# The end of a full-row product: the last two chunks taken bank by bank

## The reference

```python
x = layer_norm(DN_ALPHA * x + mix, ...)              # mix = h @ pw2_w + b; later attention @ b_wo
x = layer_norm(DN_ALPHA * x + (silu(g) * u) @ w_down + ple, ...)   # FFN_DIM 2816
h = (silu(h @ w_gate) * (h @ w_up)) @ w_down         # blocks 2: before an RMS norm
x = x + 0.5 * rms_norm(h, ff1_norm_post)
h = concat(o_diff, o_nsa) @ w_out
x = x + rms_norm(h, mix_norm_post)
```

## Time and profile before

| | |
|---|---|
| median of 3 runs | 2543.68 us (2541.88 to 2545.12) |
| the profiled execution, its own time | 2544.07 us |
| its span, first to last instruction | 2542.3 us |
| mean granted TensorE clock | 0.991 of 2.4 GHz |
| TensorE busy | 2448.5 us, 96% of the span |
| VectorE, ScalarE, GpSimd busy | 38%, 39%, 38% |

### The profile page before, as it was taken

How to read it: one execution, slowest core, us unless ns; L and a number is a source line. 1 busy time by engine, 2 the same in 40 slices (tenths; PEclk the granted TensorE clock), 3 DMA queues, 4 the chain that set the end, 5 groups by cost and what they waited for, 6 DMA issues and landing times.

```text
span 2542.3 us, 30518 instructions
## 1 busy us (share of the span) xinstructions
PE 2448.5 (96%) x11142; PEld 1930.3 (76%) x11142; DVE 953.9 (38%) x1165; ACT 981.6 (39%) x1520; POOL 968.2 (38%) x422
## 2 busy tenths in 40 slices
PE   8999999999999999999999999999899889999997
PEld 6866788888677776788888588888577656788885
DVE  6974244420422215344401433310556763333202
ACT  7754333322466634333322522222334563322212
POOL 5733444444323223444444244444232103444442
PEclk9999999999999999999999999999999999999999
DMA  4212223333111112333333133333322002223322
GB/s 144 67 41 66 88 95 99 97 93 96 61 58 59 52 57 75 94 96 99 94 96 93 56 92 98 99 91 99 124 67 67 26 1 67 90 93 99 92 98 74
DMA packets 57062, 206.70 MB, mean 81 GB/s; under 512 B 6304, under 2 KB 6304, under 8 KB 56736
## 3 DMA queue, kind: packets, MB, share of 16 engines
q1 hardware_dynamic: 56016, 199.96, 25.0%
q10 hardware_dynamic: 976, 5.77, 0.6%
HBM read 203.61 MB, written 2.10 MB: 81 GB/s over the span
## 4 chain that ended last, share of the span: by engine, by line
issue 59%; POOL 22%; PE 13%; DVE 4%; POOLq 0%; ACT 0%; DMA 0%; SPq 0%; DVEq 0%
POOL wL L370 21%; PE banks L430 4%; PE banks L431 4%; PE banks L432 4%; DVE banks L1512 2%; DMA raw<-ws 0%; POOLq L369 0%; POOL pool_sum L385 0%; DVE gpad L1496 0%; DVE banks L1507 0%; POOLq L397 0%; DVE tmp L1586 0%; DVE tmp L1594 0%; DVE tmp L1517 0%; DVE xf L1597 0%
## 5 line engine op out<-in xcount | busy, mean ns | idle before, releaser
L370 POOL TENSOR_TENSOR wL<-raw,wH 128x1024 fp32r<-128x1024 f32 x369 | 905.1, 2455 | 1524.8 <-ACT wH L948 1524.8
L430 PE MATMUL banks<-xH,wH 128*128 128x512 f32 x2104 | 832.7, 396 | 34.7 <-DVE xL L1403 11.6
L432 PE MATMUL banks<-xH,wL 128*128 128x512 f32 x2104 | 821.0, 390 | 0.0
L431 PE MATMUL banks<-xL,wH 128*128 128x512 f32 x2104 | 820.4, 390 | 0.0
L948 ACT ACTIVATE wH<-raw 128x1024 fp32r<-128x1024 f32 x371 | 392.7, 1058 | 1090.9 <-PE banks L432 1083.7
L430 PEld LDWEIGHTS banks<-xH,wH 128*128 128x128 f32 x2104 | 395.9, 188 | 137.9 <-issue 17.6
L431 PEld LDWEIGHTS banks<-xL,wH 128*128 128x128 f32 x2104 | 396.1, 188 | 83.7 <-issue 3.4
L432 PEld LDWEIGHTS banks<-xH,wL 128*128 128x128 f32 x2104 | 395.8, 188 | 84.0
L430 PE MATMUL banks<-hH,wH 128*128 (+1 forms) x704 | 276.6, 393 | 3.5 <-DVE tmp L1470 3.5
L431 PE MATMUL banks<-hL,wH 128*128 (+1 forms) x704 | 276.3, 393 | 0.0
L432 PE MATMUL banks<-hH,wL 128*128 (+1 forms) x704 | 273.9, 389 | 0.0
(11 more groups left out here) (248 smaller groups left out, 2233.0 us busy)
## 6 DMA issues: line engine op xcount, KB each, us to landing
raw<-ws SPq DMA_DIRECT2D x371, 512.0 KB, 3.5
w1b<-w ACTq DMA_DIRECT2D x2, 2048.0 KB, 11.5
xf<-xT SPq DMA_DIRECT2D x8, 256.0 KB, 7.1
out<-xf SPq DMA_DIRECT2D x8, 256.0 KB, 2.0
pf<-pT ACTq DMA_DIRECT2D x2, 512.0 KB, 4.3
con<-consts SPq DMA_DIRECT2D x1, 637.0 KB, 7.0
par<-params SPq DMA_DIRECT2D x1, 564.5 KB, 8.0
ropeT<-rope ACTq DMA_DIRECT2D x1, 512.0 KB, 4.3
```

The source lines that it names most:

```text
L370: pool.tensor_tensor(wL[:, j, :], raw[:, j, :], fp(wH[:, j, :]), ALU.subtract).then_inc(low_ready, 1)
L430: pe.matmul(bank, wH[:, slot, cols], rh, start=start, stop=False)
L431: pe.matmul(bank, wH[:, slot, cols], rl, start=False, stop=False)
L432: return pe.matmul(bank, wL[:, slot, cols], rh, start=False, stop=stop)
```

## The change

Each full-row product now leaves its last two chunks to a new function. The chunks before them run as they did. The last two are taken bank by bank: bank 0 gets the three matmuls of chunk nk-2 and the three of chunk nk-1, then bank 1, and so on. The waits for both chunks stand ahead of all of it. The two `chunk_done` signals come at bank 7, three matmuls apart. The loop has other bounds: 4 + 4 x 4 + 2 chunks in place of 1 + 5 x 4 + 1 for nk = 22, and 2 + 4 + 2 in place of 3 + 4 + 1 for nk = 8.

```diff
+TAIL = 2
...
-                def one_k(k, j, first=False, last=False):
+                def one_k(k, j, first=False):
...
-                        mm = three(ps[n][:], (slot, slice(n * P, n * P + P)), rh, rl, first, last)
-                        if last and n < 7:
+                        mm = three(ps[n][:], (slot, slice(n * P, n * P + P)), rh, rl, first, False)
+                    mm.then_inc(chunk_done, 1)
+
+                def last_chunks():
+
+                    pe.wait_ge(low_ready, c0 + nk)
+                    pe.wait_ge(ready, ready_base + nk)
+                    for n in range(8):
+                        for k in range(nk - TAIL, nk):
+                            mm = three(ps[n][:], ((c0 + k) % SLOTS, slice(n * P, n * P + P)), rH[:, k, :], rL[:, k, :],
+                                       False, k == nk - 1)
+                            if n == 7:
+                                mm.then_inc(chunk_done, 1)
+                        if n < 7:
                             mm.then_inc(bank_done, 1)
-                    mm.then_inc(chunk_done, 1)
-
-
-                before = 1 + (nk - 2) % SLOTS
-                steps = (nk - 1 - before) // SLOTS
+
+                before = 1 + (nk - 1 - TAIL) % SLOTS
+                steps = (nk - TAIL - before) // SLOTS
...
-                for k in range(before + steps * SLOTS, nk):
-                    one_k(k, k, last=k == nk - 1)
+                last_chunks()
```

## The result

The changed kernel takes 2550.55 us, median of 18 runs (2548.99 to 2554.86), and the kernel before 2543.22 us beside it (18 runs, 2540.94 to 2547.16). The ratio is 1.0028, 95% interval 1.0021 to 1.0035: slower by 0.28%, 7.3 us. The forecast was 2546.9, a change within 0.2%. The profiled execution took 2551.09 us.

The account below looks back on a forecast made before the run. TensorE, busy 2448.5 of 2542.3 us, bounds the kernel, so only tails can change. Terms -2.8 + 4.8 + 1.0 + 0.1 = +3.1 (unrounded +3.2) gave 2546.9 us; own range 2544.5 to 2548.5, 8 in 10 2542.5 to 2550.0.

Parts of the forecast that it names:

- The gains: Tails of pw2, down0, down1, down3: the mean's third sum directly follows the second, 0.65 to 0.74 us each, -2.8 in all.
- eleven operations of 0.6 to 0.7 us: Tail of down0: VectorE is late because it has these for eight banks that come complete 0.68 us apart.
- wout: Tail of wout: late rounding delays the squares, 3.6 us, and GpSimd's split stretches VectorE's first add, 1.2: 4.8 lost.
- down2: Tail of down2: ScalarE waits for the product's end anyway; the split holds the first add slightly, 0.1 us lost.
- the weights' slack: Last two chunks, waited for together: 1.7 us of slack left, cost 0; rival of late weights, 2549, chance 0.03.
- wo: Tail of wo: the late DMA of pf delays the mean's subtraction, 1.0 us lost; 2.0 if slower, 0 at best.
- The clock: Rival: TensorE's new gaps behind wout and wo's mean bring half clock, up to 2.6 us each; slower, chance 0.17.
- spaced sums have slack: Argument against the clock rival: half clock on TensorE's spaced sums in the tails need not cost time.
- the slower DMA: Upper end of the range: the DMA of pf in wo slower by as much again, 2.0 us lost.

Follow-up runs that it names:

- the signal alone: The kernel before, own order of matmuls, with only the chunk_done of chunk nk-2 given two matmuls before each full-row product's end: 2558.74 against 2543.79 us, ratio 1.0058.
- the squares put first: The changed kernel with ScalarE's last rounding of wout put behind its eight squares: 2543.30 against 2543.99 us, ratio 0.9996.
- the held split with the clock kept up: The changed kernel with dummy matmuls in TensorE's gaps at wout and wo, and GpSimd's split behind wout held back: 2545.74 against 2543.78 us, ratio 1.0007.
- the early load: The changed kernel with the DMA of pf issued ahead of wo's chunk stream: 2546.43 against 2543.99 us, ratio 1.0009.
- the run with the split held back: The changed kernel with GpSimd's split at the end of wout held until VectorE's third add of squares: 2549.46 against 2543.79 us, ratio 1.0019.
- both repairs: The changed kernel with wout's squares ahead of ScalarE's last rounding and the load of pf ahead of wo's chunks: 2539.23 against 2543.99 us, ratio 0.9977.
- kept busy: The changed kernel with 20 dummy matmuls in TensorE's gap behind wout and 18 behind the mean of wo: 2547.37 against 2543.99 us, ratio 1.0018.

## Why the prediction was wrong

*The gains* (-2.8): right in size, and the reason is only half right. -0.75, -0.84, -0.83 and -0.78 make -3.2, each 0.1 more than forecast: between its third sum and L494, TensorE took 0.96 us for 0.86 us of work before (657.22 to 658.18 in down0), and this is gone too. The prediction put VectorE's lateness down to eleven operations of 0.6 to 0.7 us. It overlooked that one of them was longer, in pw2, down0, wo and down1 alike. In down0 before:

```profile
650.60 2.42 POOL L370 TENSOR_TENSOR wL<-raw,wH 128x1024 fp32r<-128x1024 f32 x1 [3.01 <-ACT wH L948]
...
652.13 1.43 DVE L1385 TENSOR_TENSOR tmp<-xf 128x512 f32<-128x512 f32 x1
...
658.18 1.88 PE L494 MATMUL banks<-xf,con 128*128 128x512 f32 x4
```

GpSimd's split stretches VectorE's first pair sum from 0.68 to 1.43 us. In the run with the signal alone, same order of matmuls, no split lies there:

```profile
653.24 0.68 DVE L1392 TENSOR_TENSOR tmp<-xf 128x512 f32<-128x512 f32 x1
```

Its third pair sum starts 1.20 us behind the last matmul, and 1.96 before. Without the stretch the third pair sum of the earlier trace rows would have ended near 656.4, just in time for TensorE at 656.48 (an estimate from these rows). So in the layer norm tails most of the gain is the end of that meeting; in down3, where no split is near, the reason given holds. The size came out right because it was read from TensorE's rows and did not depend on the reason. That holding the split would give the same gain in the old order was not run.

*wout* (+4.8): right, +4.68, and both parts of it are shown: the hold by the squares put first, the 1.2 us of the split by the held split with the clock kept up.

*down2* (+0.1) and the weights' slack: right. No stop inside the last 48 matmuls of a product shows.

*wo* (+1.0): the step was right, and 0.3 short at full clock: the subtraction starts 6.84 us behind the last matmul, 5.56 before, so +1.28. From the issue of the DMA to `pH` it took 5.22 us, not 4.95. The other 1.69 of its +2.97 is the clock.

*The clock, which the sum had at 0 and the rivals at 0.17*: this is the step that failed. At full clock the tails add up to -3.2 + 1.28 + 0.09 + 4.68 = +2.85, close to the forecast sum of +3.2. The measured 7.3 has 4.5 more. I had argued from one gap, down2's, where the fall of the clock was free because VectorE set the pace, and that spaced sums have slack. In wo the fall lay on sums that ScalarE and TensorE pace, and there it cost 1.69 us: the profile shows it, and it is gone both when the gap is filled and when the early load shortens it. The rival had up to 2.6 us for each of the two places. In wout's own tail it was free, as argued, until the run with the split held back, where it lasted into L539's sums. Down2's gap isn't always free either, as the profile with both repairs shows.

The other 2.8 us are not shown to that degree. In the profile they lie between the tails (2.5 us), in stretches of half clock behind gaps that the change left as long as they were: 2.19 us ahead of the matmuls that follow `ple`, 2.79 behind down1, 2.49 behind wout. In the profile before, the first of the two gaps of 2.19 was followed by a stretch at half clock (near 293 us) and the second wasn't, and in the profile after it was the other way round (near 1035 us). The pass behind wout began at the half clock in the changed kernel, in two kernels whose stall in wout was gone or filled (squares first, kept busy) and in two whose stall was left (the load ahead, the signal alone); it did not in the kernel before and the other five. Such places move about 1.6 us from run to run. One profile of each kernel does not tell how often each place falls; only the medians do, and by them filling the two gaps takes back 3.9 us, give or take 3. How the new gaps bring more half clock further on stays open, and so does whether they do.

The bounds of the prediction's own range don't quite follow from its terms: 1.0 and 1.2 below 2546.9 is 2544.7, and the slower DMA 1.0 above it is 2547.9, where it has 2544.5 and 2548.5. It doesn't bear on the miss.

## What to carry to other kernels

A completion signal usually has more than one listener: before delaying it, read in program order what stands behind each wait on it, on every engine, and whether a transfer is among it. Here a reordering worth 4.8 us became a loss of 7.3, because the signal that frees a weight slot also stood ahead of two urgent pieces of ScalarE's work; moving those two ahead of it was worth 12.1. A third such piece, in down2, had stood behind the stream before the change as well, and moving it gave 7.2 more. A new gap on TensorE has to be priced twice: for its length, and for the clock behind it. In wo the second price was 1.7 us, where TensorE paced the work; in the changed kernel's sums behind wout, where VectorE did, it was nothing.

## What the runs showed of the hardware

In the places read here, a 128x512 VectorE operation on two SBUF inputs that meets a GpSimd split of 2.3 to 2.6 us ends 0.55 us behind the split's end, wherever it started: 0.7 us alone, it took 1.43 in down0 before (started 1.5 us behind the split), 1.91 in wout after, 2.80 in down0 with the signal alone, 2.43 for the first of the two of `pL` (3.03 is both). Additions that read PSUM were not stretched: 0.69 us each beside the same split. In 'SBUF: two separate sides' the Trainium skill's page 'SBUF — State Buffer' describes this as a lock; what the trace adds is the 0.55 us.

Gaps of TensorE of the same length don't always end alike. Behind down1 it idled 2.79 us before and after; the mean clock from 1417 to 1421 was 1.00 before and 0.58 after. Behind wout it idled 2.49 us in both (to 2150.90 and to 2157.01); the clock stayed at 1.00 before and fell after. The gaps of 3.46 to 3.76 us in the tails of down2, wo and wout, sixteen over the eleven profiles, were all followed by the half level. Filling the two gaps of 3.5 us with bf16 matmuls kept the sums that follow at full clock, in wo and in wout.
